# One decay matrix and a first inverse on GpSimd in the gated delta stage of a two-block model

## The reference, cut to what matters

```python
decay = jnp.cumsum(g, -1)
dmask = jnp.exp(jnp.where(incl, decay[..., :, None] - decay[..., None, :], -jnp.inf))
a_strict = jnp.where(strict, beta[..., None] * kk * dmask, 0.0)
t_mat = a_strict + jnp.eye(c)
u, w = solve(t_mat, v * beta), solve(t_mat, k * (beta * jnp.exp(decay)))
qk = (q @ k.T) * dmask
v_new = u - w @ s
o = (q * jnp.exp(decay)) @ s + qk @ v_new
s = s * exp(decay_last) + (k * jnp.exp(decay_last - decay)).T @ v_new
```

## Time and profile before

| | us |
|---|---|
| runs | 2791.17, 2787.60, 2790.86 (median 2790.86) |
| the profiled execution | 2789.88 |
| its span | 2788.1 |
| TensorE busy / VectorE / ScalarE / GpSimd | 2655.6 / 993.7 / 962.5 / 1198.9 |
| granted TensorE clock, mean | 0.948 of 2.4 GHz |
| the delta stage, from start to last copy | 1466.4 to 1649.4 |

### The profile page before, as it was taken

How to read it: one execution, slowest core, us unless ns; L and a number is a source line. 1 busy time by engine, 2 the same in 40 slices (tenths; PEclk the granted TensorE clock), 3 DMA queues, 4 the chain that set the end, 5 groups by cost and what they waited for, 6 DMA issues and landing times.

```text
span 2788.1 us, 48968 instructions
## 1 busy us (share of the span) xinstructions
PE 2655.6 (95%) x17354; PEld 2339.9 (84%) x17354; DVE 993.7 (36%) x1788; ACT 962.5 (35%) x2226; POOL 1198.9 (43%) x1007
## 2 busy tenths in 40 slices
PE   7999999999989999999996759999999899999998
PEld 7767888888767888889995759999999767999998
DVE  3253211221243221246446643432432443441340
ACT  4383222332484322233231123222233464322231
POOL 4544444444663444444333114444443432444443
PEclk9999999999999999999897979999999756999999
DMA  4222222222331222232120002222222100222222
GB/s 161 79 47 76 95 99 91 94 95 88 83 56 53 98 98 90 90 115 76 68 76 16 1 1 76 90 96 85 90 91 84 39 1 23 89 86 96 83 99 82
DMA packets 80380, 213.11 MB, mean 76 GB/s; under 512 B 30224, under 2 KB 32912, under 8 KB 80272
## 3 DMA queue, kind: packets, MB, share of 16 engines
q1 hardware_dynamic: 80272, 211.69, 22.8%
HBM read 209.57 MB, written 2.10 MB: 76 GB/s over the span
## 4 chain that ended last, share of the span: by engine, by line
PE 90%; DVE 5%; issue 2%; ACT 1%; POOL 1%; DVEq 0%; DMA 0%; POOLq 0%; ACTq 0%; SPq 0%
PE ps L1086 76%; PE ps L1317 3%; PE ps L1235 3%; PE ps L1218 2%; PE ps L1205 2%; DVE s_sb L1479 1%; PE ps L1101 1%; PE ps L1239 1%; PE ps L1287 1%; POOL bias_sb L618 1%; ACT s_sb L830 0%; DVE x_t L1454 0%; DVE s_sb L1454 0%; DVE x_m L1454 0%; DVEq L1432 0%
## 5 line engine op out<-in xcount | busy, mean ns | idle before, releaser
L540 POOL TENSOR_TENSOR w_lo<-raw,w_hi 128x512 fp32r<-128x512 f32 (+1 forms) x704 | 977.7, 1410 | 1216.9 <-ACT w_hi L731 1216.8
L1086 PE MATMUL ps<-h_hi,w_hi 128*128 128x264 f32 (+1 forms) x3392 | 905.6, 322 | 15.4 <-POOL h_lo L685 8.1
L1086 PE MATMUL ps<-h_lo,w_hi 128*128 128x264 f32 (+1 forms) x3392 | 903.4, 322 | 0.0
L731 ACT ACTIVATE w_hi<-raw 128x512 fp32r<-128x512 f32 (+1 forms) x704 | 426.5, 653 | 1381.4 <-PE ps L1086 1362.9
L1086 PE MATMUL ps<-h_hi,w_lo 128*128 128x264 f32 (+1 forms) x3392 | 901.0, 321 | 0.0
L1086 PEld LDWEIGHTS ps<-h_hi,w_hi 128*128 128x128 f32 x3392 | 567.7, 189 | 68.3 <-issue 17.1
L1086 PEld LDWEIGHTS ps<-h_lo,w_hi 128*128 128x128 f32 x3392 | 564.4, 189 | 48.3 <-issue 1.0
L1086 PEld LDWEIGHTS ps<-h_hi,w_lo 128*128 128x128 f32 x3392 | 565.0, 189 | 46.6
L1086 PE MATMUL ps<-act_lo,w_hi 128*128 128x264 f32 (+1 forms) x1056 | 282.3, 322 | 0.0
L1086 PE MATMUL ps<-act_hi,w_lo 128*128 128x264 f32 (+1 forms) x1056 | 282.0, 321 | 0.0
L1086 PE MATMUL ps<-act_hi,w_hi 128*128 128x264 f32 (+1 forms) x1056 | 280.9, 320 | 0.0
(11 more groups left out here) (224 smaller groups left out, 2396.6 us busy)
## 6 DMA issues: line engine op xcount, KB each, us to landing
raw<-slabs_d SPq DMA_DIRECT2D x288, 512.0 KB, 3.2
raw<-slabs_d SPq DMA_DIRECT2D x64, 704.0 KB, 4.0
rpb_raw<-rpb_d SPq DMA_DIRECT2D x24, 224.0 KB, 5.0
bias_sb<-alibi_d SPq DMA_DIRECT2D x6, 384.0 KB, 4.0
x<-x_d SPq DMA_DIRECT2D x1, 2048.0 KB, 12.7
out_d<-x SPq DMA_DIRECT2D x1, 2048.0 KB, 7.4
mem_in<-mem_d SPq DMA_DIRECT2D x1, 1024.0 KB, 8.6
dn_cst<-dn_consts_d SPq DMA_DIRECT2D x1, 640.0 KB, 5.0
```

The source lines that it names most:

```text
L540: nc.gpsimd.tensor_tensor(w_lo[:, s, a * P:b * P], raw[:, s, a * P:b * P], w_hi[:, s, a * P:b * P].bitcast(f32), ALU.subtract).then_inc(lo ...
L731: nc.scalar.activation(w_hi[:, s, a * P:b * P], raw[:, s, a * P:b * P], ACT.Copy)\
L1086: last = nc.tensor.matmul(ps[:, s * 2 * BANK + po:s * 2 * BANK + po + n], w[:, s, wk], a[:, k, to:to + n], start=(k == 0 and w is w_hi and ...
```

## The change

It rewrites the delta stage:

- One decay matrix: the difference of rows and column is made once, straight from PSUM, ScalarE takes its absolute value and exp(-|d|), and GpSimd multiplies it by the triangular matrix for the k by q product. The masks of -1e30 are gone; a_t's upper part is cut by the masks of the levels, which are there anyway.
- The first inverse: GpSimd makes x_t from a_t in two steps, TensorE turns it, ScalarE copies the result to x_m.
- Copies and the spread of the gates go from VectorE to ScalarE, the copies of a_t and o among them.
- The tail: GpSimd multiplies k and q by the rows' exponential (k_era, q_era); TensorE makes k_era by the state minus v in one accumulated product, with a negative identity; v_new's sign is turned in its copy.
- TensorE's other products are spread over the pieces: k by k in piece 1, k by q in 2, the turn of a in 3, the turn of x_t in 5; the turn of k in piece 1, the state's product in 4.
- GpSimd walks the rounds too, and splits one gated tile a round, in rounds 1 to 4; w_lo of the next stage's first slabs comes last.

The plan of steps, and the tiles:

```diff
-    pre = dict(pe=["rows", "dcol", "kk", "kq", "at"],
-               dve=["gb", "row", "dcol", "dlast", "dt", "dtm", "dl", "dlm", "a1", "a", "qk", "at",
-                    "x1", "x", "xt1", "xt"],
-               act=["erow", "edec", "elast", "edt", "edl"])
-    tail = dict(pe=["vt", "ks", "kt", "vn", "o", "s"],
-                dve=["bed", "r1", "r2", "r", "kd", "qd", "s1", "s", "o"], act=["vn"])
+    pre = dict(pe=["rows", "dcol", "kk", "kq", "at", "xm"], dve=["dcol", "d", "dlast", "a1", "a", "qk"],
+               act=["gb", "erow", "elast", "abs", "e", "at", "xm"], pool=["em", "first", "xt"])
+    tail = dict(pe=["vks", "kt", "vn", "o", "s"], dve=["res", "kd", "s1", "s"], act=["vn", "o"], pool=["ke", "qe"])
     at = {}
     for part, engines in (("pre", pre), ("tail", tail)):
         for engine, names in engines.items():
...
-        gb, row, dt_, dl_, a_m, z_m, k_dec, q_dec, state = (
+        gb, diff, e_m, em_t, a_m, z_m, k_dec, q_era, k_era, state = (
             small(n, four, f32, 0 if n == "gb" else None)
-            for n in ("gb", "row", "dt_", "dl_", "a_m", "z_m", "k_dec", "q_dec", "state"))
+            for n in ("gb", "diff", "e_m", "em_t", "a_m", "z_m", "k_dec", "q_era", "k_era", "state"))
...
         res, v_new = big("res", four, f32, wide_at[0] + 20 * TOK), big("v_new", four)
-        r1 = q_dec
-        after_eq, before = (dn_cst[:, i * P:(i + 1) * P] for i in range(2))
-        level_mask = [dn_cst[:, (2 + i) * P:(3 + i) * P] for i in range(LEVELS + 1)]
```

`rounds()` also gives `mid`, the chunk of the round in all six pieces. GpSimd:

```diff
-                pool.wait_ge(ba_done, 1)
+            def gated_split(st, m):
                 for s in range(RING):
                     pool.wait_ge(acc_free[s], st.slab0 // 2)
...
+                nc.gpsimd.tensor_copy(h_hi[st.h][:, m, :], conv_y[:, m, :]).then_inc(gated_hi, 1)
+                pool.wait_ge(gated_hi, m + 1)
+                nc.gpsimd.tensor_tensor(h_lo[st.h][:, m, :], conv_y[:, m, :], h_hi[st.h][:, m, :].bitcast(f32),
+                                        ALU.subtract).then_inc(gated_lo, 1)
             def head_split(st):
                 for j in range(4):
             def delta(st):
                 pool.wait_ge(loaded, 16 * N_LOADS + 16)
...
+                def over_heads(out, a, b, op, part):
+                    nc.gpsimd.tensor_tensor(out, a, b, op).then_inc(d_sem[part, "pool"], 1)
+                def all_heads(m, n):
+                    return m[0:n, 0:n].unsqueeze(1).to_broadcast([n, DN_H, n])
+                for here, mid, old, new, i in rounds():
+                    if here:
+                        s, n = here.levels[i], here.n
+                        if i == 0:
+                            here.after(pool, "pre", "act", "at")
+                            if here.c:
+                                past = Chunk(here.c - 1)
+                                past.after(pool, "levels", "pe", ("z", past.levels[-1]))
+                        elif i >= 2:
+                            here.after(pool, "levels", "pe", ("z", s - 2))
+                        over_heads(a_lv[0:n, s % 2, :, 0:n], here.a_t[here.sq4], all_heads(level_mask[s - 1], n),
+                                   ALU.mult, "levels")
+                    if new and i == 2:
+                        new.after(pool, "pre", "act", "e")
+                        over_heads(em_t[new.sq4], e_m[new.sq4], all_heads(tri, new.n), ALU.mult, "pre")
+                    if mid and i == 4:
+                        k = mid
+                        if old:
+                            old.after(pool, "tail", "pe", "o")
+                        over_heads(k_era[:, :, 0:k.n], qkv[:, 4:8, k.tok], k.erow[:, :, 0:k.n], ALU.mult, "tail")
+                        over_heads(q_era[:, :, 0:k.n], qkv[:, 0:4, k.tok], k.erow[:, :, 0:k.n], ALU.mult, "tail")
+                    if new and i == 5:
+                        n = new.n
+                        new.after(pool, "pre", "act", "at")
+                        over_heads(new.x_t[new.sq4], new.a_t[new.sq4], all_heads(first_level_t, n), ALU.mult, "pre")
+                        new.after(pool, "pre", "pool", "first")
+                        over_heads(new.x_t[new.sq4], all_heads(ident, n), new.x_t[new.sq4], ALU.subtract, "pre")
+                    if mid and mid.c and i == 3:
+                        gated_split(st, mid.c - 1)
+                stream(st.slab0 + 2)
             for n, st in enumerate(stages):
```

ScalarE:

```diff
+                def spread_gate(k):
+                    nc.scalar.activation(gb[0:k.n, :, :], gate[:, k.c, :][0:k.n].unsqueeze(2).to_broadcast([k.n, DN_H, P]),
+                                         ACT.Copy).then_inc(d_sem["pre", "act"], 1)
+                def level(k, s):
+                    k.after(act, "levels", "pe", ("z", s))
+                    nc.scalar.activation(z_m[k.sq4], quad(4, k.n)[0:k.n], ACT.Copy).then_inc(d_sem["levels", "act"], 1)
+                def tail(k, i):
+                    done = d_sem["tail", "act"]
+                    if i == 2:
+                        k.after(act, "tail", "pe", "vn")
+                        nc.scalar.activation(v_new[0:k.n, :, :], quad(7, P)[0:k.n], ACT.Copy, scale=-1.0).then_inc(done, 1)
+                    if i == 4:
+                        k.after(act, "tail", "pe", "o")
+                        nc.scalar.activation(qkv[:, 8:12, k.tok], quad(3, k.n), ACT.Copy).then_inc(done, 1)
+                def pre(k, i):
+                    n, done = k.n, d_sem["pre", "act"]
+                    if i == 0:
+                        k.after(act, "pre", "dve", "dlast")
+                        nc.scalar.activation(k.erow[:, :, 0:n], quad(0, n), ACT.Exp).then_inc(done, 1)
+                        nc.scalar.activation(k.elast[0:n, :], dlast[0:n, :], ACT.Exp).then_inc(done, 1)
+                    if i == 1:
+                        nc.scalar.activation(e_m[k.sq4], diff[k.sq4], ACT.Abs).then_inc(done, 1)
+                        k.after(act, "pre", "act", "abs")
+                        nc.scalar.activation(e_m[k.sq4], e_m[k.sq4], ACT.Exp, scale=-1.0).then_inc(done, 1)
+                    if i == 4:
+                        k.after(act, "pre", "pe", "at")
+                        nc.scalar.activation(k.a_t[k.sq4], quad(0, n)[0:n], ACT.Copy).then_inc(done, 1)
+                    if i == 5:
+                        k.after(act, "pre", "pe", "xm")
+                        nc.scalar.activation(k.x_m[k.sq4], quad(1, n)[0:n], ACT.Copy).then_inc(done, 1)
+                        if k.c + 1 < len(CHUNKS):
+                            spread_gate(Chunk(k.c + 1))
+                act.wait_ge(gate_made, 1)
+                spread_gate(Chunk(0))
+                for here, _, old, new, i in rounds():
                     if here:
...
+                        level(here, here.levels[i])
+                    if old:
+                        tail(old, i)
+                    if new:
+                        pre(new, i)
```

TensorE:

```diff
                     if first:
-                        k.after(pe, "pre", "dve", "xt")
+                        k.after(pe, "pre", "act", "xm")
                         if k.c:
...
-                        turn(quad(7, P)[0:n], lambda h: qkv[:, 8 + h, k.tok], P).then_inc(done, 1)
+                        k.after(pe, "tail", "pool", "qe")
+                        pe.wait_ge(gate_made, 3)
                         if k.c:
-                            Chunk(k.c - 1).after(pe, "tail", "dve", "o")
-                        heads(quad(3, P)[0:n], lambda h: qkv[:, 4 + h, k.tok], lambda h: state[:, h, :]).then_inc(done, 1)
+                            Chunk(k.c - 1).after(pe, "tail", "dve", "s")
+                            Chunk(k.c - 1).after(pe, "tail", "act", "o")
+                        for h in range(DN_H):
+                            nc.tensor.matmul(quad(3, P)[0:n, h, :], k_era[:, h, 0:n], state[:, h, :],
+                                             start=True, stop=False)
+                            last = nc.tensor.matmul(quad(3, P)[0:n, h, :], qkv[:, 8 + h, k.tok], neg_ident[:, :],
+                                                    start=False, stop=True)
+                        last.then_inc(done, 1)
+                    if i == 1:
                         turn(quad(2, P)[0:n], lambda h: qkv[:, 4 + h, k.tok], P).then_inc(done, 1)
                     if i == 2:
-                        k.after(pe, "tail", "dve", "r")
+                        k.after(pe, "tail", "dve", "res")
                         k.after(pe, "levels", "dve", ("xt", k.levels[-1]))
                         heads(quad(7, P)[0:n], lambda h: k.x_t[0:n, h, 0:n], lambda h: res[0:n, h, :]).then_inc(done, 1)
                     if i == 3:
-                        k.after(pe, "tail", "dve", "qd")
                         k.after(pe, "tail", "act", "vn")
                         for h in range(DN_H):
-                            nc.tensor.matmul(quad(3, n)[:, h, :], state[:, h, :], q_dec[:, h, 0:n], start=True, stop=False)
```

(35 more changed lines are left out.)

97 lines of the change are left out of this document (18 added, 79 removed).

## The result

The changed kernel takes **2753.7 us** (median of 2756.80, 2751.30, 2717.48 and 2756.09), beside 2789.7 for the kernel before (median of four). The ratio is 0.985 with an interval of 0.980 to 0.989. The ratio is built from all runs, the one of 2717 us among them. The profiled execution took 2756.8 us (span 2755.0). Beside the profiled one of before, 2789.88, that is 33.1 us less; the sum in the prediction was 33.5.

The account below looks back on a forecast made before the run. Rounds were held bound by VectorE's queue at their end and each level's TensorE-ScalarE-VectorE loop before. Gains of 4.6, 7.0, 8.5 twice, 3.3 and 1.6 us sum to 33.5: 2789.9 - 33.5 + 1 = 2757.4, said as 2757; range 2748 to 2770.

Parts of the forecast that it names:

- walk of the rounds: Delta stage, piece by piece: full round 37.5 to 29.0 us, round 0 21.7 to 17.1, round 4 24.1 to 20.8.
- GpSimd's steps of the inverse: First inverse's steps on GpSimd, in no row of the profile: between 1.27 and 1.79 us each, taken as 1.27.
- Round 1: Delta stage: 38.1 us to 31.1, made of 29.0, 1.4 for a low-clock start and 0.7 for the narrow old chunk.
- end of the stage: From level 6 to the last copy, 16.2 us before: copy done at 14.6, a gain of 1.6 us.
- steps up to chunk 0's first level: Start of the delta stage: one hop more on ScalarE and GpSimd, fewer on VectorE; gain 0.
- new wait: Piece 1: ScalarE's rows' exponential, waiting for dlast, stands ahead of level 2's copy and delays it, 1.7 us a round.
- last step of the sum: Whole kernel: profiled execution 2789.9 us, less 33.5 gained, plus 1 for the median of the runs, gives 2757.4.
- A: Low clock after piece 1's gap: three groups at 0.89 us more in three rounds, 8 us, giving 2765; chance 0.13.
- B: GpSimd sets a round's end, at 1.79 us a step: 1.5 to 3 us a round, giving 2764; chance 0.10.
- C: Level 2's copy doesn't wait: 1.7 us less in three rounds and 1 in round 0, giving 2751; chance 0.05.
- D: TensorE granted 1.2 GHz at every level within the rounds; slower, 2805 with 60% of that work at it; chance 0.05.
- E: Round's end no shorter, a seven-step chain over four engines: a full round falls by 4 us only, 2777; chance 0.07.

Follow-up runs that it names:

- seven idle products: Changed kernel plus seven 512-column TensorE products that do no useful work, ahead of the third and fourth pair of the last attention: 2708.5 us, ratio 0.9689.
- seven late idle products: Changed kernel plus seven useless 512-column TensorE products in the middle of the last attention (second group, third pair), not at its start: 2723.6 us, ratio 0.9758.
- execution with the rise at 2263: One execution, 2736.4 us, of the changed kernel with GpSimd's four subtractions at the last attention's start set apart, no product added; that version's median is 2754.3 us.

## Why the prediction was right and where it failed

**The walk of the rounds was right.** Full rounds: 29.0 predicted, 29.20 measured, twice. Round 4 up to level 6: 20.8 and 20.9 (1586.40 to 1607.30, the copy at 1608.47 less 1.17). Round 0: 17.1 and 17.9. The wait at a round's end is 0.73 us for ScalarE's x_m, "about 1" in the text. GpSimd's steps of the inverse took 1.27 us, the lower bound, which I took. Abs took 0.63 us with no table load, and the page of the Trainium skill that I named there (ScalarE: Activation LUTs, "Table sets: the hidden batching unit") agrees with the trace.

**Two terms were mis-sized and three left out, and that they cancel is luck.** Round 1 took 34.4 us, not 31.1. I had given its start at low clock 1.4 us, and the table by stretch shows two stretches at the lower level:

```profile
1493.60:1498.60 5.00, 5.00 (x23) 3.90 (x24) 0.00 (x0) 1.01 (x2) 1.74 (x2) 0.50 0.00 0
1498.60:1515.60 17.00, 15.40 (x128) 14.22 (x126) 7.88 (x13) 4.10 (x8) 5.60 (x5) 1.00 0.00 1
1515.60:1519.00 3.40, 3.40 (x17) 3.36 (x17) 0.69 (x1) 0.00 (x0) 2.84 (x3) 0.51 0.00 0
```

Ahead of the second one TensorE did not stand still at all; what stands there are the narrow products of the 16-token chunk's o. In the profile of the changed kernel with seven idle products this second stretch is missing, and round 1 takes 32.8 us at a clock of 0.93. So part of the miss varies from run to run.

The end of the stage gained 4.2 us (16.24 to 12.08), not 1.6. I had left the product of res and x_t at the lower level, and the products of o behind it (v_new at 10.0, o at 13.8). They ran at the higher one: 1.16 us where the first took 2.08, and 2.1 for o where I had 3.8. Behind it the norm gained 2.0 us (23.0 to 21.0, from the last copy's end to the projection), which no term held: its first column sums take 2.05 us where they took 3.63. The steps up to chunk 0's first level, put at 0, gained 0.6: from the start of the last products ahead of the stage they take 7.7 us where they took 8.4. Yet the stage begins 1.4 us later, because those last products start 2.0 us later (1467.94, before 1465.91). They come ahead of every step that the change touches, and over the profiles of the changed kernel and its variants they start anywhere from 1462.9 to 1471.8: this is variation between executions, which no term held either.

By these cuts 3.8 + 3.7 + 8.2 + 8.3 + 3.2 + 4.2 + 2.0 + 0.6 is 34.0 us; less the 2.0 ahead of the stage, with 1.1 found behind it, it is the 33.1 measured. It lies 0.4 from the 33.5 of the sum with single terms off by up to 3.3.

**The new wait** was sized at 1.7 us a round and is 1.4; taking it away shortened the round by 1.39.

**What failed is a term that was not there.** The last step of the sum, "2789.9 - 33.5 + 1 = 2757.4", and the range around it treat the rest of the kernel as one time. It is not: TensorE's granted clock in the attention has two courses, worth 49 to 52 us from end to end, and an execution can leave the lower one on the way. The run of 2717.48 us stands 34 to 39 us below its neighbours at a mean clock of 0.973 (they read 0.952 to 0.954). That is what a rise of the clock early in the attention would give: 49 us over some 144 at the lower level are a third of a microsecond for each, so 39 us are some 115 us spared. The profiled execution with the seven late idle products, whose clock rises at about 2200, took 2722.9 us at the same mean clock. Nor is there room for it elsewhere, by an estimate from the clocks: a mean of 0.952 over 2755 us leaves 132 us missing to full clock, 76 of them in the attention (0.53 over the 162 us from 2158 to 2320) and 56 in the rest; at 0.973 over 2716 us only 73 are missing, 59 fewer. Still, this run left no profile, so for it the cause is argued and not shown. The execution with the rise at 2263 is the shown case of the same kind, and one run of the kernel before at 2776.3 us (clock 0.956) beside six of 2787 to 2798 fits. The four runs of the result held one such run, and it is what took the ratio times 2789.7 below 2748: the other three have a mean of 2754.7. I had put this stretch at a clock of 0.50 in neither sum nor rivals, since both kernels have it; a range for a ratio of few runs has to hold it.

**The rivals.** A (low clock in piece 1) did not come in rounds 2 and 3; low clock beyond a round's start came in round 1 alone, and not in piece 1. B: GpSimd's last step was done before the turn could start. C: the copy did wait. D is ruled out by the clock of 1.00 in rounds 2 and 3. E would have left 33 us a round. The Trainium skill (TensorE: Matmul & The Clock Gate, "A second HAM failure mode: psum-queue depth-cycling") tells of a kernel whose clock swung because of short idle times between groups of matmuls; read as a rule, it would have made the clock swing here. Rounds 2 and 3 stood at 1.00 with idle times of 0.7 and 1.6 us in them, so for these rounds the trace disagrees. The clock reads 0.90 or 0.91 in the rounds where 3.0 us or more stand at their end (the first inverse on VectorE, the copies on VectorE, the kernel before). But the length of an idle time alone doesn't decide it: with the products bunched it fell behind 0.95 and 0.73 us, and in round 1 behind none.

**The parts, each undone alone** (ratio less that of the changed kernel, times 2797): copies on ScalarE 19 us, first inverse by GpSimd 15, products spread 8, gated tiles one a round about 1, not told from nothing. These add up to 43 us beside a gain of 37, so they are not independent: undoing either of the first two brings back 3 to 5 us of idle time at a round's end and the low clock behind it, and both counts hold that.
